# One block of samples goes first: 256 gathered rows move from the expert stage into the heads stage

## The reference

```python
def trunk_layer(x, c, pos0, C0, n0, m0, S0, w_ada, ...):
    mod = jax.nn.silu(c) @ w_ada + b_ada
    sh1, sc1, g1, sh2, sc2, g2 = jnp.split(mod[:, None, :], 6, axis=-1)
    h = layer_norm(x) * (1.0 + sc1) + sh1
    mix, st = token_mixers(h, pos0, C0, n0, m0, S0, w_in, b_in, head_g, w_out)
    x = layer_norm(ALPHA * x + g1 * mix, ln1_g, ln1_b)
    h = layer_norm(x) * (1.0 + sc2) + sh2
    x = layer_norm(ALPHA * x + g2 * peer(h, w_pq, sub_keys, expert_u, expert_v), ln2_g, ln2_b)
    return x, st
```

```python
    s = jnp.einsum("phcd,cnd->phcn", q, sub_keys)
    sv, si = lax.top_k(s, PEER_TOPK)                     # 16 of 128, for both halves of the key
    tv, ti = lax.top_k(cand, PEER_TOPK)                  # 16 of the 16 x 16 sums
    g = jax.nn.softmax(tv, axis=-1)
    u = jnp.take(expert_u, eidx, axis=0)
    act = jax.nn.gelu(jnp.einsum("phkd,pd->phk", u, xt))
    return jnp.einsum("phk,phkd->pd", g * act, jnp.take(expert_v, eidx, axis=0))
```

## Time and profile before

| | us |
|---|---|
| median of 3 runs | 3932.34 (3927.49 to 3935.54) |
| the profiled execution | 3938.18 |
| its span, from the first instruction to the last | 3936.5 |
| PE busy in the span | 3294.2 (84%) |
| DVE busy | 2919.7 (74%) |
| POOL busy | 1882.0 (48%) |
| ACT busy | 993.1 (25%) |
| gathers by POOL (queue q0) | 555.83 MB, 37.4% of 16 DMA engines' span |
| other transfers (queue q1) | 315.50 MB, 25.0% |

### The profile page before, as it was taken

How to read it: one execution, slowest core, us unless ns; L and a number is a source line. 1 busy time by engine, 2 the same in 40 slices (tenths; PEclk the granted TensorE clock), 3 DMA queues, 4 the chain that set the end, 5 groups by cost and what they waited for, 6 DMA issues and landing times. The chain is left out here.

```text
span 3936.5 us, 48738 instructions
## 1 busy us (share of the span) xinstructions
PE 3294.2 (84%) x16909; PEld 2635.9 (67%) x16909; DVE 2919.7 (74%) x5949; ACT 993.1 (25%) x1966; POOL 1882.0 (48%) x1654
## 2 busy tenths in 40 slices
PE   8669999995857878773799999899999999999992
PEld 1535554442327777773688888888888888888881
DVE  1523333333875787889899999899999999999986
ACT  0101110112002888840222222222222222222220
POOL 0000000000110999940777667676677767777650
PEclk9589999997978999986899999999999999999996
DMA  7221112102122343330999999999999999999983
GB/s 265 84 59 36 36 40 55 48 6 91 70 97 88 89 97 91 91 92 11 365 377 368 365 368 372 355 381 354 373 368 379 373 352 373 369 370 371 348 314 139
DMA packets 456246, 873.94 MB, mean 222 GB/s; under 512 B 196302, under 2 KB 245710, under 8 KB 455895
## 3 DMA queue, kind: packets, MB, share of 16 engines
q0 software_dynamic: 153008, 555.83, 37.4%
q1 hardware_dynamic: 303032, 315.50, 25.0%
HBM read 808.07 MB, written 63.15 MB: 221 GB/s over the span
## 5 line engine op out<-in xcount | busy, mean ns | idle before, releaser
L1498 POOL DMA_INDIRECT ring<-in_expert_u,experts x512 | 717.6, 1402 | 398.8 <-POOLq L1041 148.1
L1498 POOL DMA_INDIRECT ring<-in_expert_v,experts x512 | 684.0, 1336 | 295.7 <-DVE acc L1629 167.5
L1629 DVE SCALAR_TENSOR_TENSOR acc<-ring,wgt,acc 128x1024 f32<-128x1024 f32 x508 | 651.2, 1282 | 22.3 <-DMA ring<-in_expert_v,experts 1.5
L1620 DVE CUSTOM_DVE_ANT_1 ring<-ring,h2T 128x1024 f32<-128x1024 f32 x512 | 613.5, 1221 | 31.2 <-DMA ring<-in_expert_u,experts 30.2
L670 PE MATMUL z<-W,hT 128*128 128x512 f32 x1152 | 508.2, 595 | 20.9 <-DMA bh<-in_b_in 20.9
L1514 PE MATMUL a<-h2T_hi,uhi 128*128 128x320 f32 x2048 | 362.9, 322 | 188.9 <-ACT w L1583 99.3
L1263 POOL TENSOR_SCALAR hotJ<-cst,pickT 128x128 f32<-128x128 f32 x560 | 424.5, 776 | 124.7 <-ACT pickT L1250 120.2
L1514 PEld LDWEIGHTS a<-h2T_hi,uhi 128*128 128x128 f32 x2048 | 327.2, 197 | 202.0 <-issue 103.8
L670 PEld LDWEIGHTS z<-W,hT 128*128 128x128 f32 x1152 | 214.9, 191 | 265.3 <-issue 265.3
L1514 PE MATMUL a<-h2T_lo,uhi 128*128 128x320 f32 x2048 | 363.6, 323 | 0.0
L1514 PE MATMUL a<-h2T_hi,ulo 128*128 128x320 f32 x2048 | 349.1, 314 | 0.0
(11 more groups left out here) (276 smaller groups left out, 5174.2 us busy)
## 6 DMA issues: line engine op xcount, KB each, us to landing
ub<-in_expert_uT SPq DMA_DIRECT2D x128, 512.0 KB, 6.7
vf<-in_expert_v SPq DMA_DIRECT2D x128, 512.0 KB, 9.6
weight_d<-stage SPq DMA_DIRECT2D x10, 4096.0 KB, 20.9
wt<-weight_d SPq DMA_DIRECT2D x128, 320.0 KB, 8.0
wa<-in_w_ada SPq DMA_DIRECT2D x12, 2048.0 KB, 8.1
W<-in_w_in SPq DMA_DIRECT2D x32, 512.0 KB, 8.3
wq<-in_w_pq SPq DMA_DIRECT2D x4, 2048.0 KB, 19.7
ring<-in_expert_u,experts POOLq DMA_INDIRECT x512, 7.7
```

Of the source, the lines that this page charges most:

```text
L1498: pool.indirect_dma_start(ring[:, r, :], None, table, bass.IndirectOffsetOnAxis(experts[:, gb, k % SLOTS:k % SLOTS + 1], 0)).then_inc(land ...
L1620: dve.tensor_tensor_reduce(u, u, h2, 1.0, 0.0, ALU.mult, ALU.add, dots[:, k:k + 1]).then_inc(used, 1)
L1629: dve.scalar_tensor_tensor(dst, src, wk, dst, ALU.mult, ALU.add).then_inc(used, 1)
```

## The change

The sample block runs alone first, through heads, output and routing; then the prompt's eight blocks run through the heads, and in their 64 steps the 256 gathers of the sample block are done, four in a step. The expert stage keeps the 768 gathers of blocks 5 to 7. `mixer_phase` is split for it: `norm_gate_phase` (the norm and the gates, for all blocks, as before) and `heads_phase`, which takes the blocks it works on and is written out without loops; `output_phase` and `routing_phase` take their blocks too. The weights of the heads, of the output and of the queries are loaded once for each of the two passes.

```diff
+        with semaphores(nc) as sem:
+            modulation_phase(nc, a, sem, mod_d, cst, ones, const)
         with ExitStack() as mid:
-            mixer_phase(nc, a, o, sem, mod_d, cst, ones, const, hB, gB)
-            output_phase(nc, a, sem, mod_d, x1_d, h2_d, const, hB, gB)
+                with semaphores(nc, "s_") as sem:
+                    norm_gate_phase(nc, a, o, sem, mod_d, cst, ones, const, mix)
+                    heads_phase(nc, a, o, sem, ones, const, mix, hB, gB, (SB,))
+                    output_phase(nc, a, sem, mod_d, x1_d, h2_d, const, hB, gB, (SB,))
+                with semaphores(nc, "s_") as sem, nc.sbuf_tensor("h2T_one", [P, KC, P], F32) as h2T:
+                    wq = heads_out[:, 0:NP, :, :].rearrange("p b g d -> p b (g d)")
+                    routing_phase(nc, a, sem, h2_d, weight_d, const, h2T, experts, gates, (SB,), 0, wq)
+                with semaphores(nc) as sem:
+                    heads_phase(nc, a, o, sem, ones, const, mix, hB, gB, PROMPT, Early(SB, experts, gates, h2_d, gath_d))
+            with semaphores(nc) as sem:
+                output_phase(nc, a, sem, mod_d, x1_d, h2_d, const, hB, gB, PROMPT)
...
+                routing_phase(nc, a, sem, h2_d, weight_d, const, h2T, experts, gates, PROMPT, ND)
```

`heads_phase`, SP: the weights of a head, then for the sample block the states:

```diff
+            for hd in range(2 * H):
+                hh, grp, h = hd % 2, hd // H, hd % H
+                if hd >= 2:
+                    sp.wait_ge(z_done, NS * (hd - 1))
+                    sp.wait_ge(z_taken, NS * (hd - 1))
+                for j, part in enumerate(ORDER):
+                    lo = (RET0 if grp else 0) + part * MW + h * DH
+                    sp.dma_start(W[:, hh, :, j, :], ...).then_inc(w_in_[hh], 16)
+                    sp.dma_start(bh[:, hh, j, :], ...).then_inc(w_in_[hh], 16)
+                if sampled:
+                    if hd >= 2:
+                        sp.wait_ge(stored[hh], stored_by(hd - 2))
+                    sp.dma_start(Cs[:, hh, :, 0:DH], ...).then_inc(cs_in[hh], 16)
...
+            if early:
+                sp.wait_ge(used, 2 * SLOTS)
+                sp.dma_start(early.gath_d[...], acc[:, :]).then_inc(kept, 16)
+                sp.wait_ge(kept, 16)
```

POOL: four gathers a step (`PER`) into a ring of four (`RING`), then the state of a head that is done:

```diff
+            for n, (hd, b) in enumerate(STEPS):
+                if early:
+                    for i in range(PER * n, PER * (n + 1)):
+                        if i >= RING:
+                            pool.wait_ge(used, i - RING + 1)
+                        pool.indirect_dma_start(ring[:, i % RING, :], None, table_d, ...).then_inc(landed[i % RING], 16)
+                if b == NP - 1:
+                    pool.wait_ge(c_ready, n + 1)
+                    pool.dma_start((S_p if grp else C_p)[0, 0, h, :, :], C[:, hh, 0:DH]).then_inc(stored[hh], 16)
```

DVE: `gathered(i)` waits for row i to land and takes it as in the expert stage (a dot product for the first 128, a weighted sum for the others), at four places of a step:

```diff
                 dve.tensor_scalar(kw[:, pb, :], k, wend, None, ALU.mult).then_inc(kw_ready, 1)
+                if early:
+                    gathered(PER * n)
                 dve.wait_ge(s_done, n + 1)
...              (pm)
+                if early:
+                    gathered(PER * n + 1)
                 dve.wait_ge(inter_ready, n + 1)
...              (hB, then the state C)
+                if early:
+                    gathered(PER * n + 2)
+                    gathered(PER * n + 3)
```

The expert stage's pace: 10, 10, 2 and 2 gathers in the key rows of a group, 24 in all, where a key row does not cross a multiple of 128:

```diff
-    PACE = {0: (2, 2, 2, 1, 3, 2), 1: (2, 2, 2, 1, 3, 2), 2: (1, 1, 1, 1, 0, 0), 3: (1, 1, 1, 1, 0, 0)}
+    gone_by = []
+    for n in range(NK):
+        last = gone_by[-1] if n else 0
+        want = 6 * (n // GS * GS) + (10, 20, 22, 24)[n % GS]
+        gone_by.append(min(want, (last // SLOTS + 1) * SLOTS))
```

More of the change, by code:

```diff
@@ L572, in mixer_phase @@
[L572 to L593, removed]
@@ L595, in weights @@
-            def weights(hh, grp, h):
-                base = RET0 if grp else 0
-                for j, part in enumerate(ORDER):
[L598 to L619, removed]
-                            sp.dma_start(Cs[:, hh, :, DH:VW],
-                                     a["state_mlstm_n"][0, :, bass.ds(h, 1), :].rearrange("b h d -> d (b h)").unsqueeze(2),
-                                     allow_slow_non_contiguous=True).then_inc(cs_in[hh], 16)
-                rounds(sp, body)
@@ L838, in output_phase @@
-def output_phase(nc, a, sem, mod_d, x1_d, h2_d, const, hB, gB):
+            Cs = sb2("Cs", [P, 2, SEQS, VW])
+        else:
+            C = sb2("C", [P, 2, VW])
+        if early:
+            ring = sb2("e_ring", [P, RING, D])
+            h2e = sb2("e_h2", [P, D])
+            acc = sb2("e_acc", [P, D])
+            dots, wgt = sb2("e_dots", [P, SLOTS]), sb2("e_wgt", [P, SLOTS])
+            landed = [sem(f"e_l{i}") for i in range(RING)]
+            h2e_in, used, wgelu_done, wgt_ready, kept = (
+                sem("e_h2"), sem("e_used"), sem("e_wg"), sem("e_wr"), sem("e_kept"))
@@ L944, in _ @@
         def _(pe):
-            for b in range(NB):
+            for b in range(NL):
                 pe.wait_ge(y_ready, b + 1)
@@ L1674, in _, with part @@
                 taken = g and s < 2
-                pace = PACE[s]
-                gathers(pace[0])
+                first, more = at[0], gone_by[n] - at[0]
+                def part(tenths):
+                    gathers(first + more * tenths // 10)
+                part(2)
                 if n + 1 < NK:
@@ L1681, in _ @@
                         split_v(n + d)
-                gathers(pace[1])
+                part(4)
                 multiply(n, 0)
-                gathers(pace[2])
+                part(6)
                 multiply(n, 1)
-                gathers(pace[3])
+                part(7 if taken else 10)
                 split_w(n)
@@ L1689, in _ @@
                     take(g - 1, 3 * s)
-                gathers(pace[4])
+                part(9 if taken else 10)
                 if taken:
                     take(g - 1, 3 * s + 1)
-                gathers(pace[5])
+                part(10)
                 if taken:
```

741 lines of the change are left out of this document (392 added, 349 removed).

## The result

The changed kernel takes 4100.2 us (median of 4 runs, 4093.1 to 4109.0) against 3933.3 (4 runs): a ratio of 1.043, 95% interval 1.040 to 1.046. It is slower, as forecast, and by 167 us instead of 97. The profiled execution has a span of 4104.0 us, 167.5 above the one before.

What follows compares the result with a forecast made beforehand. DVE was taken to hold back PE in the expert stage, PE to bound the heads. Terms -165 + 251 - 82 + 68 - 27 + 97 - 48 + 3 = +97 gave 4030 us from the median; 8-in-10 range 3940 to 4150.

Steps and rivals of the forecast that it cites:

- lone output and lone routing: Sample block's own passes through output and routing: +68 us (bounds 62 and 85) and +97 us (bounds 90 and 110).
- the signs: Prompt heads: steps of 9.0 us, DVE busy above 90%, waiting for landings only beside weight loads and at heads' first steps.
- the forecast's own 3985 to 4080: Whole kernel: the forecast's own range, chance 0.56, with sample heads 226 to 283, expert -140 to -180, prompt heads -114 to -50.
- the prompt heads: Heads stage of the prompt's blocks: 64 steps instead of 72, 655 us against 736.6 before, -82.
- 18 for late ones: Prompt heads: 18 us added for gathered rows landing late beside the six later weight loads.
- 14 for POOL's stores: Prompt heads: state stores wait for C ahead of the next four gathers, about 2 us late, 7 times, 14 us.
- 20.1 and 24 us: First weight loads before PE starts: 20.1 us in the sample heads, 24 in the prompt heads with four gathers beside them.
- 62 us for a pair: Sample heads: a pair of heads chained by SP's queue, 62 us, 50 with retention states; 251 us in all.
- the transfers that are never late: Rival, both heads passes: weights and states always in time, sample heads 151, prompt heads 623, kernel 3898 us; chance 0.10.
- the expert stage that keeps half its stops: Rival, expert stage: ub waits for its single buffer, saving 85 us instead of 165, kernel 4110 us; chance 0.11.
- The ring of four: Rival, prompt heads: ring too short, each row 2.4 us late as rows and weights share DMA engines, 4152 us; chance 0.12.
- Half clock throughout: Rival, sample block's lone links: PE at half clock for all of each link, +70 us, kernel 4100 us; chance 0.07.

## Why the prediction was right, and where its size was off

The reading held: DVE held the expert stage back, PE the heads, and the price of the second pass exceeds what it frees. The groups came out at 55.4 us against PE's 55.7 from the earlier trace rows; lone output and lone routing at 67 and 97.5 against 68 and 97. DVE waited for rows almost only beside weight loads and at the heads' begins, as the signs said. The time lies in the range of 3940 to 4150, but above the forecast's own 3985 to 4080, because the prompt heads left their band (-20, not -114 to -50).

The term that was mis-sized is the prompt heads, at "18 for late ones" and 14 for POOL's stores. With 5 for the last rows that is 37 us; the rows cost 101. I priced lateness by the median landing of the earlier trace rows, and took the heads' thin traffic for a reason that most rows are in time. Most are (median 5.6 us). But the rows at a head's end meet 2 MB of weights in 512-byte packets and, on POOL's own way, the 128 single elements of n. The 14 for POOL's wait for C was near (15 in the run with the store behind the rows); what n's store does to the rows behind it I had not counted. DVE's load was off too: in a settled step it waits for the scores for 1.45 us in an mLSTM head and for 0.8 in a retention head, the kind that I had read, so it is busy for 82% of the one and 88% of the other, and for 68% of the stage.

The second is the first load of each pass. I took 20.1 and 24 us from the earlier trace rows; PE started 37.2 and 41.2 us after the begins, 17 us later in both. In the sample heads that is all of the miss. In the prompt heads 12 of the 17 are there without rows too, and they do not show in the sum, because other terms of that stage were some 14 us too long: without rows it took 615.9 and not 623 + 12 - 5, since the second projection was counted beside the steps. So 64 for the rows, 12 for the load and 14 less make the 62. The load of the earlier trace rows, with nothing else under way, was no fixed price: the same bytes came at about half the speed, and the cause stays open.

The sample heads' 62 us for a pair was near: by the short products of heads 0, 2, 4 and 6 the pairs took 61.5, 58.8 and 54.9 us against 62, 62 and 50. The cause is less so. SP does wait for the stores, as forecast, but putting the state's load behind the weights gave 12 us alone; the weights take that long anyway.

Of the rivals, the transfers that are never late is out, and so is the expert stage that keeps half its stops, although its 4110 lay nearer to the time than 4030 did. The ring of four is half right: it is too short at the head ends only, and a longer one doesn't cure it. Half clock throughout is out as well, and that its 4100 was met is luck: a sample projection after a wait of 5 us and more took 9.2 to 10.1 us, one after 1.3 us 7.1, and none the 13.9 that 1.2 GHz throughout would make of 6.95 (granted on the mean of the stage: 0.71). The loss is at each projection's start: after such a wait its products first follow each other in 0.85 to 1.0 us, and from the sixth to the eighth of the sixteen on in 0.43. The Trainium skill, "TensorE: Matmul & The Clock Gate", section "HAM oscillation — how this bites in real kernels", says that a PE that waits for a transfer ahead of every tile starts each tile at the lower clock. This trace agrees as far as these starts go.

## What to carry to other kernels

When work moves into another stage's idle time, look not at the mean step but at the stage's seams: which bursts and which small stores share the queue and the transfer engines with the new work there. And what a second pass over weights costs depends on how they are fetched: wide, early, and into room that is free just then, the sample heads took 146 us instead of 266, and with the seams mended the same move of the rows went from 4.3% slower to 2.3% faster.

## What the hardware showed that was not expected

- A store of 128 single elements on POOL's way held up a gathered row behind it: 11.3 us from issue to use, against 4.3 behind a store of whole rows (with the weights' loads left out).
- The loads of head 0 came in packets of 31 to 39 ns before the change and of 81 to 101 ns after it (means of a load), also in third place of the order (82 to 95); the other heads' took 38 to 62. Neither the rows nor the form of the address caused it.
- SP took 59.8 us to issue 8 MB as 16 transfers in 512-byte packets and 16.7 us as 4 transfers in packets of 2 KB.
